# Loading the second token tile of x through ScalarE's DMA queue, ahead of the small vectors

## The reference

```
shift, scale, gate = split(c @ W_ada + b_ada)         # c: one vector of 2048; W_ada 2048 x 6144
h = RMSNorm(x, g_pre) * (1 + scale) + shift           # x: 256 x 2048
p = h @ W_in                                          # W_in 2048 x 11328, split into q, kv-latent, rope key,
                                                      # diff q, k, v, two gates, two merge gates
A = MLA(p) * silu(gate_A) @ W_oA ;  B = DiffAttn(p) * silu(gate_B) @ W_oB
y = (sigmoid(g_A) * A + sigmoid(g_B) * B) @ W_out
out = x + gate * RMSNorm(y, g_post)
```

## Time and profile before

| | us |
|---|---|
| median of 3 runs | 766.39 |
| the profiled execution | 766.48 |
| its span, first to last instruction | 764.6 |
| TensorE busy | 753.4 |
| VectorE busy | 562.4 |
| ScalarE busy | 418.6 |
| packets of SP's DMA queue, share of 16 engines | 75.8% |

### The profile page before, as it was taken

One profiled execution on the slowest core, in us unless ns is written; L12 is line 12 of the kernel. 1 busy time (PEld: TensorE's weight loads), 2 busy tenths in 40 slices (PEclk: granted clock), 3 DMA queues, 4 the chain that ended last, 5 costly groups with the idle time before them and its releaser, 6 DMA issues.

```text
span 764.6 us, 10080 instructions
## 1 busy us (share of the span) xinstructions
PE 753.4 (99%) x3681; PEld 624.4 (82%) x3681; DVE 562.4 (74%) x825; ACT 418.6 (55%) x612; POOL 21.4 (3%) x95
## 2 busy tenths in 40 slices
PE   7999999999999999999999999999999999999997
PEld 5777788888888988888888888888888888888885
DVE  4898999889868579889887778676554556465554
ACT  5678777665567554544545565655444444444441
POOL 2000000000000000000000000011100000000001
PEclk9999999999999999999999999999999999999999
DMA  9999999999674789888886575555566656567642
GB/s 337 395 392 395 381 394 345 355 358 294 190 221 122 212 282 301 295 274 285 285 291 195 164 217 183 163 174 161 178 186 193 192 174 210 179 211 248 220 163 110
DMA packets 132555, 189.71 MB, mean 248 GB/s; under 512 B 10325, under 2 KB 68122, under 8 KB 132250
## 3 DMA queue, kind: packets, MB, share of 16 engines
q1 hardware_dynamic: 132240, 188.77, 75.8%
q10 hardware_dynamic: 266, 0.30, 0.1%
HBM read 185.90 MB, written 2.10 MB: 246 GB/s over the span
## 4 chain that ended last, share of the span: by engine, by line
PE 87%; DMA 6%; DVE 2%; issue 2%; ACT 2%; SPq 1%; DVEq 0%; ACTq 0%
PE ps L1911 17%; PE ps L1913 17%; PE ps L1912 17%; PE ps L1901 11%; PE ps L1870 8%; PE ps L1887 6%; DMA w_raw<-in_w_in 4%; PE ps L1873 4%; DMA ada_ring<-in_w_ada 1%; PE ps L1706 1%; ACT w_both L1035 1%; SPq L525 1%; DVE ada_acc L1311 1%; PE ps L1691 1%; PE ps L1721 1%
## 5 line engine op out<-in xcount | busy, mean ns | idle before, releaser
L1559 DVE TENSOR_TENSOR w_both<-w_raw,w_both 128x1024 fp32r<-128x1024 f32 x248 | 301.7, 1222 | 159.7 <-ACT w_both L1035 158.4
L1035 ACT CAST w_both<-w_raw 128x1024 fp32r<-128x1024 f32 x248 | 259.3, 1050 | 245.9 <-PE ps L1913 183.7
L1901 PE MATMUL ps<-w_both,h_both 128*128 128x512 f32 x560 | 138.7, 390 | 0.0
L1901 PEld LDWEIGHTS ps<-w_both,h_both 128*128 128x128 f32 x560 | 105.0, 188 | 22.5 <-DVE w_both L1559 0.4
L1911 PE MATMUL ps<-w_both,h_both 128*128 128x512 f32 x296 | 116.8, 395 | 0.0
L1913 PE MATMUL ps<-w_both,h_both 128*128 128x512 f32 x296 | 115.4, 390 | 0.0
L1912 PE MATMUL ps<-w_both,h_both 128*128 128x512 f32 x296 | 115.2, 389 | 0.0
L1887 PE MATMUL ps<-w_both,h_both 128*128 128x512 f32 x280 | 76.2, 394 | 1.0 <-ACT h_both L991 0.7
L1311 DVE SCALAR_TENSOR_TENSOR ada_acc<-ada_ring,cols,ada_acc 128x512 f32<-128x512 f32 x98 | 69.6, 745 | 0.5
L1911 PEld LDWEIGHTS ps<-w_both,h_both 128*128 128x128 f32 x296 | 55.6, 188 | 12.6 <-issue 1.7
L1913 PEld LDWEIGHTS ps<-w_both,h_both 128*128 128x128 f32 x296 | 55.6, 188 | 11.7
(11 more groups left out here) (268 smaller groups left out, 844.0 us busy)
## 6 DMA issues: line engine op xcount, KB each, us to landing
w_raw<-in_w_in SPq DMA_DIRECT2D x177, 512.0 KB, 4.6
ada_ring<-in_w_ada SPq DMA_DIRECT2D x128, 256.0 KB, 6.4
gate_ring<-in_w_ada SPq DMA_DIRECT2D x32, 512.0 KB, 5.2
w_raw<-in_w_out SPq DMA_DIRECT2D x32, 512.0 KB, 3.8
w_raw<-in_w_o_mla SPq DMA_DIRECT2D x16, 512.0 KB, 3.8
w_raw<-in_w_o_diff SPq DMA_DIRECT2D x16, 512.0 KB, 4.1
w_raw<-in_w_ukv SPq DMA_DIRECT2D x16, 256.0 KB, 3.3
x_tok<-in_x SPq DMA_DIRECT2D x2, 1024.0 KB, 6.0
```

Source lines behind the costliest of these rows:

```text
L1035: act.copy(w_hi[:, p % RING, :], w_raw[:, p % RING, :]).then_inc(hi_done, 1)
L1559: dve.tensor_tensor(w_lo[:, p % RING, :], w_raw[:, p % RING, :], w_hi[:, p % RING, :].bitcast(F32), ALU.subtract).then_inc(lo_done, 1)
L1901: ins = mm(ps[:, b0 + t, :], lhsT=side[:, 2 * i + r, t * P:(t + 1) * P], rhs=w[:, p % RING, r * CH:(r + 1) * CH], start=False, stop=last a ...
```

## The change

SP issues only tile 0 of x. Tile 1 is issued by ScalarE, as the first instruction of its program, ahead of the five small loads. Semaphores, destination, source and everything that waits are the same.

```diff
         @block.sync
         def _(sp):
-            for t in range(TOK):
-                sp.dma_start(x_tok[:, t, :], x[0, t * P:(t + 1) * P, :]).then_inc(x_in[t], 16)
+            sp.dma_start(x_tok[:, 0, :], x[0, 0:P, :]).then_inc(x_in[0], 16)
             def load_ada(j, q):
...
         @block.scalar
         def _(eng):
+            eng.dma_start(x_tok[:, 1, :], x[0, P:TOK * P, :]).then_inc(x_in[1], 16)
             eng.dma_start(vec_rows[V_C:V_C + KT, :], c[0, :].rearrange("(r n) -> r n", n=P)).then_inc(vec_in, 16)
```

## The result

The changed kernel takes 768.08 us (median of 9 runs, 767.44 to 769.16) against 766.42 us (9 runs, 765.92 to 766.76): a ratio of 1.0026, 95% interval 1.0017 to 1.0034. It is slower by 1.7 us, just outside the predicted range (765.1 to 768.0 us) and on the side of the slower rival. The profiled execution took 768.03 us, span 766.2 us.

The account below looks back on a forecast made before the run. Bytes moved by DMA were taken to bound the kernel up to 68.86 us, TensorE's work the rest. From 766.5 us: issue 0, ramp 0, tile 0 +1.4, slack -1.4, vectors 0; forecast 766.4 us, range 765.1 to 768.0 us.

Parts of the forecast that it names:

- slower rival: Opening: tile 0's lag is not absorbed because the slack lies in VectorE's gaps; 767.8 to 768.1 us, chance 0.18.
- landing of tile 0: Start of the kernel: tile 0 of x shares the engines with tile 1, landing at 8.0 instead of 5.6 us.
- slack of 1.63 us: TensorE from piece 0 to piece 17: time to spare against the loads, taken to absorb the 1.4 us lag.
- Piece 17's load: End of the load-bound stretch: still lands at about 68.9 us, as its latency shrinks when issued later.
- small vectors: ScalarE's five small loads: the last awaited to 9.0 us, between 8.6 and 10.3 us, at cost 0.
- the issue: SP's queue: later issues may come 0.43 us earlier; worth taken as 0, bounds 0 and -0.43 us.
- the ramp: DMA between 1 and 3 us: a second queue might fill it; taken as 0, range 0 to -0.6 us.
- the transposes and the four filler matmuls then end at 20.55 instead of 18.80 us: TensorE's opening: the transposes of x start 1.75 us later, at 11.45 us, and end later by as much.
- +1.4 (tile 0): Term of the sum: tile 0's later landing starts piece 0 at 24.2 instead of 22.81 us.
- VectorE was mis-sized: VectorE's opening rows: slot 0 ends at 12.4 us and slot 1 follows at once, +0.9 us, less than TensorE's lag.
- deciding point: TensorE's opening: tile 0's lag is not absorbed once piece 0 starts later than 24.44 us, or earlier if VectorE is tighter.
- forecasts of 72.0 us for the start of piece 17 and of 394 GB/s: Load-bound stretch to about 68.9 us: piece 17 starts on TensorE at 72.0 us as before, DMA still moving 394 GB/s.

Follow-up runs that it names:

- fillers over the gap: Changed kernel with seven instead of four filler calls ahead of the vectors' transpose on TensorE and two more behind it; 766.47 us, ratio 1.0002.
- half of tile 1: Changed kernel with only half of x's tile 1 in ScalarE's queue, the other half behind tile 0 in SyncE's; 768.04 us, ratio 1.0023.
- fewer fillers: Kernel before the change with two instead of four filler calls at the start of TensorE's program, loads as before; 766.48 us, ratio 1.0003.
- tile 1 first: Kernel before the change with its two x loads in the other order, both on SyncE's queue; 768.46 us, ratio 1.0028.
- long lag: Kernel before the change with ten instead of two filler calls between x's transposes and the closing of the first modulation sums; 771.19 us, ratio 1.0064.
- vectors first with fillers: Changed kernel with the small vectors ahead of tile 1 in ScalarE's queue, and fillers in each of TensorE's opening waits; 766.71 us, ratio 1.0007.
- shorter lag: Kernel before the change with six instead of two filler calls between x's transposes and the closing of the first modulation sums; 767.72 us, ratio 1.0021.
- tile 1 behind slot 0: Kernel before the change, all on SyncE's queue, with tile 1 of x issued behind the two loads of W_ada's slot 0; 766.44 us, ratio 1.0003.

## Why the prediction was wrong

**What held.** The landing of tile 0 was named as the cost, and the two queues do share the engines almost evenly: 67 packets of SP's queue and 59 of ScalarE's move between 1 and 5 us of the changed kernel,

```profile
q1 hardware_dynamic: 67, 0.55, 41.8%
q10 hardware_dynamic: 59, 0.48, 32.1%
```

The slack of 1.63 us, worked out from rows 3 and 8, measured 1.55 to 1.62 us in the ten runs with larger lags. Piece 17's load landed at 69.0 us where 68.9 us was forecast, by a shorter time from issue to landing (5.9 us for 8.0 us), as the prediction had it. The small vectors cost nothing (awaited to 9.4 us, taken as 9.0 us, needed by 11.4 us). Neither the issue nor the ramp brought anything: 49, 213 and 352 GB/s in the second to fourth microsecond, 614 together, against 66, 169 and 429, 664 together; the second profile of the changed kernel has 98, 147 and 328, 573 together.

**What failed.** The step "the transposes and the four filler matmuls then end at 20.55 instead of 18.80 us", which moved L1811 by 1.75 us and kept its 7.39 us. It moved by 2.15 us and took 9.01 us, so they ended 3.77 us late. The term of the sum that failed is "+1.4 (tile 0)": it measured 3.16 us, 1.76 us more. The clock makes 1.62 us of that, a landing at 8.28 us where 8.0 us was taken 0.28 us (the bound that the prediction itself gave), issue and waiting up to the first transpose 0.12 us; 0.26 us come back at L1622, which starts 0.16 us before the fillers' modelled end and whose first eight matmuls take 1.05 instead of 1.16 us. By the same sum without the clock's 1.62 us, an estimate, piece 0 would have been 1.54 us late, just within the slack, and the forecast time would have stood; the run with fillers over the gap, 1.82 us late and 0.23 us of it paid, bears that out. VectorE was mis-sized too, without effect on the time: its rows of slots 2 to 7 start at 14.56 instead of 13.05 us, 1.51 us late and not 0.9, because `make_diag(1)` at 14.34 us waited 0.45 us for GpSimd. The prediction looked at what TensorE waits for and not at what it does meanwhile: the row that it needed was the pair of 3.1 us of wait before 9.70 us and clock 1.00 behind it, with a kernel that carries fillers for just this. That row could have raised the question; that 4.7 us of wait would cost the clock only the runs showed.

**The slower rival** had the right sign and nearly the right size (767.8 to 768.1 us) but the wrong mechanism: it said that the slack would not be usable. The slack was used in full; the lag was larger, and that 3.16 us less 1.57 us comes near the rival's 1.4 to 1.7 us is luck. Its deciding point, piece 0 after 24.44 us, did decide: 25.97 us.

The forecasts of 72.0 us for the start of piece 17 and of 394 GB/s failed with the lag: piece 17 starts at 73.93 us though its load is there at 69.0 us, since TensorE, over 1.57 us late, now sets the pace, and the stretch moves 385 GB/s.

## What to carry to other kernels

Two loads of 1 MB issued within 0.01 us from two queues landed here at 8.3 and 8.5 us, where one behind the other on one queue they landed at 5.6 and 8.3 us. So before sharing, ask which of them the first consumer needs, and whether it can do anything with the second before the first is through. A lag is paid only beyond the slack against the resource that sets the stretch, and that slack can be worked out ahead from two starts and an undisturbed pace. Where a change lengthens a wait of TensorE, look at the granted clock behind it, and stretch the fillers with the wait; and compare several executions, since one profile shows one fall.

## What was not expected of the hardware

In the profiles TensorE's granted clock stayed at 1.00 behind a wait of 3.1 us (with one 0.25 us matmul in it) and went to 0.50 in or behind waits of 4.0 us (half of tile 1), 4.4 us (fewer fillers), 4.7 us (changed) and 5.1 us (tile 1 first). The length of the wait does not settle it: with fewer fillers, five of eleven executions had a mean granted clock of 1.000. How long it stays down differs from one execution to the next of the same kernel: 3.4 us of L1811 in one profile of the changed kernel, from before 10 us to past 16 us in another. Three of the kernels whose profile shows the clock up repeat within 0.2 to 0.7 us (long lag, fillers over the gap, vectors first with fillers); the changed kernel and the two with tile 1 first or in halves spread over 1.2 to 1.7 us. The shorter lag and tile 1 behind slot 0 stay within 0.3 and 0.8 us but for the one slow execution of each.

The clock's rise differs too. The table's clock column reads 1.00 from the start in every profile, but the weight loads of the first fillers (L1631) come 0.85 us apart at first and 0.43 us apart later (kernel before: 2.53, 3.38, 4.23, then 4.73, 5.16 us). The same eight filler matmuls take 5.09 us before and 5.57 us in the changed kernel, and 5.99 us in its second profile:

```profile
1.51 5.09 PE L1631 MATMUL ps<-ident 128*128 128x512 f32 x8 [1.51 <-POOL ident L610]
...
1.51 5.57 PE L1631 MATMUL ps<-ident 128*128 128x512 f32 x8 [1.51 <-POOL ident L609]
```

Without tile 1's load, which they do not touch, they took 6.49 us. So the fillers' pace, and with it the length of the wait behind them, changes from one execution to the next.
